# One 512 KB block of expert weights kept in two PSUM banks, in a decoder layer with 32 experts on Trainium2

## The reference

```
h2 = rms_norm(x) * norm2_w
logits = h2 @ w_router + b_router          # 32 experts
top 4 experts of each token, softmax over their logits
for each expert e, for the tokens that chose it:
    u = h @ w1[e] + b1[e]                  # w1: 1024 x 2048, 8 MB
    gate, lin = halves of u;  gate = min(gate, 7);  lin = clip(lin, -7, 7)
    y = (gate * sigmoid(1.702 * gate) * (lin + 1)) @ w2[e] + b2[e]    # w2: 1024 x 1024, 4 MB
    acc[token] += weight of the expert * y
out = rms_norm(x + acc) * final_norm_w
```

## Time and profile before

| | |
|---|---|
| median of 3 runs | 1038.2 us (1037.85 to 1038.82) |
| the profiled execution's own time | 1038.53 us |
| its span in the profile | 1036.7 us |
| moved by DMA | 424.64 MB, 410 GB/s over the span |
| granted clock of TensorE | 0.999 of full speed |

### The profile page before, as it was taken

How to read it: one execution, slowest core, us unless ns; L and a number is a source line. 1 busy time by engine, 2 the same in 40 slices (tenths; PEclk the granted TensorE clock), 3 DMA queues, 4 the chain that set the end, 5 groups by cost and what they waited for, 6 DMA issues and landing times.

```text
span 1036.7 us, 11300 instructions
## 1 busy us (share of the span) xinstructions
PE 1018.4 (98%) x4892; PEld 410.9 (40%) x4892; DVE 245.9 (24%) x613; ACT 126.6 (12%) x247; POOL 0.2 (0%) x4
## 2 busy tenths in 40 slices
PE   9999999999999999999999999999999999999996
PEld 8888443333333333333333333333333333333331
DVE  5776332111111111111111111110111111111111
ACT  2433120000000000000000000000000000000002
POOL 0000000000000000000000000000000000000000
PEclk9999999999999999999999999999999999999999
DMA  9983999999999999999999999999999999999995
GB/s 327 365 335 143 419 386 425 427 428 429 430 428 436 430 427 433 433 426 432 433 429 429 437 428 428 435 429 429 432 432 428 433 433 428 430 435 422 429 421 223
DMA packets 35976, 424.64 MB, mean 410 GB/s; under 512 B 3176, under 2 KB 16112, under 8 KB 19280
## 3 DMA queue, kind: packets, MB, share of 16 engines
q1 hardware_dynamic: 35616, 423.51, 97.0%
q10 hardware_dynamic: 304, 0.33, 0.1%
HBM read 422.78 MB, written 1.05 MB: 409 GB/s over the span
## 4 chain that ended last, share of the span: by engine, by line
PE 89%; DMA 9%; DVE 0%; another core or an unknown queue 0%; issue 0%; ACT 0%; DVEq 0%
PE PS L1861 39%; PE PS L1884 19%; DMA ring<-in_w 9%; PE PS L1455 6%; PE PS L1829 5%; PE PS L1811 5%; PE PS L1698 3%; PE PS L1658 3%; PE PS L1919 2%; PE PS L1821 2%; PE PS L1421 1%; PE PS L1803 1%; PE PS L1398 0%; PE PS L1991 0%; PE PS L2005 0%
## 5 line engine op out<-in xcount | busy, mean ns | idle before, releaser
L1861 PE MATMUL PS<-ring,work 128*64 128x512 f32 x1976 | 432.4, 594 | 6.6 <-DMA ring<-in_w 6.4
L1861 PEld LDWEIGHTS PS<-ring,work 128*64 128x64 f32 x1976 | 139.8, 137 | 276.2 <-issue 264.7
L1884 PE MATMUL PS<-ring,work 128*64 128x512 f32 x1024 | 227.6, 596 | 1.6 <-DMA ring<-in_w 1.5
L1884 PEld LDWEIGHTS PS<-ring,work 128*64 128x64 f32 x1024 | 72.3, 137 | 154.0 <-issue 150.0
L1301 DVE TENSOR_SCALAR work<-PS 128x512 f32<-128x512 f32 x32 | 22.1, 692 | 384.9 <-PE PS L1861 384.9
L842 ACT ACTIVATE work<-work 128x512 f32<-128x512 f32 x32 | 20.2, 630 | 523.0 <-DVE work L1301 523.0
L1266 DVE TENSOR_TENSOR work<-PS,n2w 128x512 f32<-128x512 f32 x30 | 20.7, 691 | 228.1 <-PE PS L1821 228.1
L1455 PE MATMUL PS<-ring 128*128 128x256 f32 x280 | 64.5, 382 | 0.0
L1829 PE MATMUL PS<-late,work 64*128 64x512 f32 x248 | 61.9, 616 | 0.0
L1811 PE MATMUL PS<-resid,work 128*64 128x512 f32 x248 | 58.5, 592 | 0.0
L1455 PEld LDWEIGHTS PS<-ring 128*128 128x128 f32 x280 | 51.8, 190 | 7.7 <-issue 1.3
(11 more groups left out here) (198 smaller groups left out, 455.7 us busy)
## 6 DMA issues: line engine op xcount, KB each, us to landing
ring<-in_w SPq DMA_DIRECT2D x72, 4096.0 KB, 35.7
ring<-in_w SPq DMA_DIRECT2D x35, 2048.0 KB, 13.1
ring<-in_w SPq DMA_DIRECT2D x22, 1024.0 KB, 8.4
ring<-in_w_in SPq DMA_DIRECT2D x11, 1024.0 KB, 12.1
ring<-in_w_out SPq DMA_DIRECT2D x4, 1024.0 KB, 11.1
ring<-in_w SPq DMA_DIRECT2D x6, 512.0 KB, 6.9
work<-in_w SPq DMA_DIRECT2D x1, 1024.0 KB, 9.0
out<-resid SPq DMA_DIRECT2D x3, 256.0 KB, 3.0
```

What stands on the lines that cost most here:

```text
L1861: last = mm(bank(b0 + v)[64 * half:64 * half + 64, :], rows[:, c, :], turned_half(w[:, v * F:(v + 1) * F], half), start=(second and c == 0 ...
L1884: last = mm(out[64 * half:64 * half + 64, :], aT_n[:, c, 64 * h:64 * h + 64], ring[:, 2 * d + c // 2, cols:cols + BANK], start=(h == 0 and ...
```

## The change

ScalarE copies the first 1024 columns of slot 7 (a part of g15, loaded ahead) to the PSUM banks 7 and 6. SP then loads the first 1024 columns of g16 (step 3, expert 3's w1) into that place of slot 7. When the first 1024 columns of g4 have been used, ScalarE copies the parked columns from PSUM to the first 1024 columns of slot 8, which before the change was the target of this part of g16. TensorE reads each from its new place: in `up` for g16, in `down` for g15. Chunk g27, which takes pair 3 (slots 6 and 7), waits for g16 in place of g15. To leave the banks 6 and 7 idle, the logits of the second tile go to bank 3 and the second half of the rows to bank 5. The two semaphores of the rows' copies become one.

```diff
@@ -60,10 +60,12 @@
 END_HALVES = [(LAST, W1_CHUNKS), (LAST, W1_CHUNKS + 1), (E, 0)]
 assert PEEL + ITERS * UNROLL + 2 == E and TURNS * PAIRS == UNROLL * STEP_CHUNKS
 SENTINEL = 3.0e38
-LT_BANK, LOGIT_BANK = (3, 0), (2, 6)
-ROWS0_BANK, TURN0_BANK = (4, 7), (3, 5)
+LT_BANK, LOGIT_BANK = (3, 0), (2, 3)
+ROWS0_BANK, TURN0_BANK = (4, 5), (3, 5)
+PARK_BANK = (7, 6)
 CUTS = {0: (1024, 2048), 1: (2048,), 2: (2048,), 3: (2048,), 4: (1024, 2048), 5: (2048,), 8: (2048,), 10: (2048,)}
 MOVED, AHEAD = 3, 3 + PAIRS
+GUEST, HOST = 4 + PAIRS, 4
 DEAL = 4
 WARM_X, WARM_WIN = 26, 12
 WIN0_PARTS, X_TURN_AT = [(0, 2), (2, C // 2)], C - 1
@@ -291,6 +293,8 @@
         y_last = g_sb
         gx = g_sb
         moved_w = work[:, 1280:3328]
+        lodging = ring[:, 2 * MOVED + 1, 0:2 * BANK]
+        parked_home = ring[:, 2 * HOST, 0:2 * BANK]
         y_sb = late[:, :]
         gh1 = late[:, :].rearrange("p (c s) -> p c s", c=C)
 
@@ -313,6 +317,8 @@
         early_in = {g: sem(f"early_in{g}") for g in CUTS if g != MOVED}
         moved_in = sem("moved_in")
         ahead_in = sem("ahead_in")
+        parked = sem("parked")
+        restored = sem("restored")
         x_in = [sem(f"x_in{k}") for k in range(T + 1)]
         cst_in = sem("cst_in")
         ident_in = sem("ident_in")
@@ -398,8 +404,7 @@
         pick0_ready = sem("pick0_ready")
         prefix0_done = sem("prefix0_done")
         rows0_done = sem("rows0_done")
-        rows0a_ready = sem("rows0a_ready")
-        rows0b_ready = sem("rows0b_ready")
+        rows0_ready = sem("rows0_ready")
         gather0_done = sem("gather0_done")
         rows_done = sem("rows_done")
         rows_ready = sem("rows_ready")
@@ -419,7 +424,6 @@
         fnw_mixed = sem("fnw_mixed")
         scaled = sem("scaled")
         combined = sem("combined")
-        final_ready = sem("final_ready")
         out_ready = sem("out_ready")
 
         read = {}
@@ -585,6 +589,8 @@
             sp.wait_ge(logits_done, T)
             sp.wait_ge(chunk_used, HEAD_CHUNKS)
             sp.dma_start(moved_w, moved_src).then_inc(moved_in, 16)
+            sp.wait_ge(parked, 2)
+            sp.dma_start(lodging, w1_half(3, 0)[:, 0:2 * BANK]).then_inc(early_in[HOST], 16)
 
             def load_ahead_rest(j, k):
                 sp.wait_ge(early_used, cut_count(MOVED, 0))
@@ -597,8 +603,9 @@
                 dst = ring[:, 2 * d:2 * d + 2, :].rearrange("p a n -> p (a n)")
                 at = 0
                 for n, cut in enumerate(CUTS[freed]):
-                    sp.wait_ge(early_used, cut_count(freed, n))
-                    sp.dma_start(dst[:, at:cut], src[:, at:cut]).then_inc(early_in[freed], 16)
+                    if freed != HOST or n > 0:
+                        sp.wait_ge(early_used, cut_count(freed, n))
+                        sp.dma_start(dst[:, at:cut], src[:, at:cut]).then_inc(early_in[freed], 16)
                     at = cut
                 sp.wait_ge(chunk_used, HEAD_CHUNKS + freed + 1)
                 sp.dma_start(dst[:, at:], src[:, at:]).then_inc(pair_full[d], 16)
@@ -625,8 +632,9 @@
                         sp.wait_ge(chunk_used, r * ROUND_CHUNKS + HEAD_CHUNKS)
                     else:
 
+                        freed = GUEST if isinstance(r, int) and g == AHEAD + PAIRS else g - PAIRS
                         sp.wait_ge(chunk_used, r * ROUND_CHUNKS + i * (UNROLL * STEP_CHUNKS)
-                                   + (HEAD_CHUNKS + g - PAIRS + 1))
+                                   + (HEAD_CHUNKS + freed + 1))
                     load(r, i, j, k)
 
             run_experts(sp, step_loads, 0)
@@ -814,10 +822,13 @@
                                  ACT.Copy).then_inc(h2T1a_ready, 1)
             square_x2(1, 1, 4)
             std_x2(1)
+            act.wait_ge(ahead_in, 16)
+            for n, b in enumerate(PARK_BANK):
+                nc.scalar.activation(bank(b), lodging[:, half_cols(n)], ACT.Copy).then_inc(parked, 1)
             for a in range(2):
                 act.wait_ge(rows0_done, a + 1)
                 nc.scalar.activation(gx1[0:64, a * SEQ:(a + 1) * SEQ], bank(ROWS0_BANK[a])[0:64, 0:SEQ],
-                                     ACT.Copy).then_inc(rows0a_ready, 1)
+                                     ACT.Copy).then_inc(rows0_ready, 1)
             for t in range(T):
                 act.wait_ge(top_ready, t + 1)
                 nc.scalar.activation(expl[:, t, :], logits[:, t, 0:E], ACT.Exp,
@@ -840,6 +851,10 @@
                 if j < E:
                     act.wait_ge(gate_ready, n + 1)
                     nc.scalar.activation(s_sb, g_sb, ACT.Sigmoid, scale=ALPHA).then_inc(sig_ready, 1)
+                if isinstance(r, int) and j == 0:
+                    act.wait_ge(early_used, cut_count(HOST, 0))
+                    for h, b in enumerate(PARK_BANK):
+                        nc.scalar.activation(parked_home[:, half_cols(h)], bank(b), ACT.Copy).then_inc(restored, 1)
                 if j < LAST and not (isinstance(r, int) and j == 0):
                     take_rows(n + 1)
                 if j == LAST:
@@ -1326,7 +1341,7 @@
 
                 dve.wait_ge(rows0_done, a + 1)
                 nc.vector.tensor_copy(gx1[64:P, a * SEQ:(a + 1) * SEQ],
-                                      bank(ROWS0_BANK[a])[64:P, 0:SEQ]).then_inc(rows0b_ready, 1)
+                                      bank(ROWS0_BANK[a])[64:P, 0:SEQ]).then_inc(rows0_ready, 1)
 
             def take_gather0(half, a):
 
@@ -1791,8 +1806,7 @@
             for a in range(2):
                 gather0_rows(1, a).then_inc(rows0_done, 1)
             bias0_part(1).then_inc(bias_done, 1)
-            pe.wait_ge(rows0a_ready, 2)
-            pe.wait_ge(rows0b_ready, 2)
+            pe.wait_ge(rows0_ready, 4)
             for a in range(2):
                 turn_rows0(a)
 
@@ -1854,8 +1868,10 @@
                         moved = first and q == MOVED and c % 2 == 1
                         if moved:
                             pe.wait_ge(moved_in, 16)
-                        w = moved_w if moved else ring[:, 2 * d + c % 2, :]
                         for v in range(2):
+                            w = moved_w if moved else ring[:, 2 * d + c % 2, :]
+                            if isinstance(r, int) and g == GUEST and c % 2 == 0 and v == 0:
+                                w = lodging
                             for half in range(2):
                                 at = v * F + half * BANK
                                 last = mm(bank(b0 + v)[64 * half:64 * half + 64, :], rows[:, c, :], turned_half(w[:, v * F:(v + 1) * F], half),
@@ -1875,14 +1891,15 @@
                         transpose_gates()
                         bias(1, 2, False)
 
-            def down_part(j, k, c0, c1, aT_n, out):
+            def down_part(j, k, c0, c1, aT_n, out, lodged=None):
 
                 d, h = pair_of(j, k), down_chunk(j, k)
                 for c in range(c0, c1):
                     for half in range(2):
                         cols = (c % 2) * D + half * BANK
+                        w = parked_home if c == lodged else ring[:, 2 * d + c // 2, :]
                         last = mm(out[64 * half:64 * half + 64, :], aT_n[:, c, 64 * h:64 * h + 64],
-                                  ring[:, 2 * d + c // 2, cols:cols + BANK],
+                                  w[:, cols:cols + BANK],
                                   start=(h == 0 and c == 0), stop=(h == 1 and c == 3))
                 return last
 
@@ -1898,7 +1915,8 @@
                     down_part(j, k, 0, 2, aT, bank(5)).then_inc(early_used, 1)
                     down_part(j, k, 2, 4, aT, bank(5)).then_inc(chunk_used, 1)
                     return
-                down_part(j, k, 0, 4, aT, bank(5)).then_inc(chunk_used, 1)
+                lodged = 2 if isinstance(r, int) and g == AHEAD else None
+                down_part(j, k, 0, 4, aT, bank(5), lodged).then_inc(chunk_used, 1)
 
             def down_first(r, j, k):
 
@@ -1993,6 +2011,7 @@
 
             def transpose_gates():
                 pe.wait_ge(most_ready, 1)
+                pe.wait_ge(restored, 2)
                 for t in range(T):
                     last = nc.tensor.transpose(bank(7)[0:E, t * P:(t + 1) * P], gates[:, t, 0:E], ident)
                 last.then_inc(gatesT_done, 1)
```

## The result

The changed kernel takes 1041.02 us (median of 12 runs, 1040.39 to 1042.84) against 1038.22 for the kernel before (12 runs beside it, 1037.72 to 1039.86). The ratio is 1.0022, with a 95% interval of 1.0014 to 1.0029: 2.3 us slower by the ratio (1.5 to 3.0), 2.8 by the medians. The forecast was 1040.9, a loss of 2.7.

A forecast was written before the change was run, and what follows sets the result against it. The prediction took the loads of weights (DMA time) to set the end. Its terms, 0 for parking, return, banks and SP plus 2.7 us for the late g27, gave 1041.2, or 1040.9 us against the runs' median; range 1038.9 to 1041.9.

The forecast's parts named there:

- my three rows: 2 MB landings into an idle queue: 7.2 us (at 100.9), 8.1 (at 131.2), 7.9 (built from 66.9); 7.7 taken.
- Parts 1 and 3: ScalarE's two parking copies near 133.5 us and two return copies near 157, covered by idle time or slack: 0.
- Part 5: After g28 the DMA queue has work to the end, so the 2.7 us loss stays; TensorE catches up before 808.
- The chain's long piece of loads: Sign in the changed kernel's profile: it begins before 808 us and the last weights land near 1020.3.
- Part 2: SP's early 512 KB load at about 134.9 us fills the dip at 141: 0 to 1.23 us earlier behind it.
- part 4: g27 issued at 216.69, 7.3 us late, empties the queue; g28 lands 2.7 us late, bounds 2.2 and 3.1.
- The first rival: At the wait of g27, an idle queue lands 2 MB nearer 7.0 us: loss 2.0, 1040.2 us; chance 0.11.
- The other rivals: At g27: the 1.2 us gain kept, 1037.0 us, chance 0.05; or the late load hidden, 1038.2, chance 0.06.

The follow-up runs named there:

- the repeat: The changed kernel run and profiled once more, against the kernel before: 1040.69 us, ratio 1.0016.
- late1: The kernel before with one line changed, g27 waiting for g16 in place of g15, nothing parked: 1040.63 us, ratio 1.0018.
- split_cols: The changed kernel with g27 loaded in three parts, only the 512 KB under g16's borrowed place waiting for its matmuls: 1038.75 us, ratio 0.9999; once more 1038.3, 0.9997.
- guest_cols: The changed kernel with g27 waiting only for the first four matmuls of g16, which read the borrowed place: 1039.38 us, ratio 1.0004.
- copies: The changed kernel without the early load and the later wait of g27; parking, return and moved banks stay: 1038.64 us, ratio 1.0002.
- more halves: The kernel split_cols with g18, g19, g21 and g23 also issued in two 1 MB halves: 1038.72 us, ratio 0.9998 against the kernel before.
- drop: The kernel before without the 512 KB load of g16's first 1024 columns at 156.5 us: 1038.16 us, ratio 0.9993.
- Extra: The kernel copies with an additional early 512 KB load that nobody reads, g16 still loaded whole later: 1038.23 us, ratio 0.9997 against the kernel before.

## Why the prediction was right

**Right in the cause, and in the sum within its bounds.** The forecast was one term, 2.7 us with bounds of 2.2 and 3.1, at one wait, that of g27. Measured are 2.3 us by the ratio (1.5 to 3.0), and 1.7 in the repeat (0.6 to 2.6); the wait alone (late1) makes 1.9, a longer wait 6.1, and without the wait (split_cols) nothing is left of the loss. The landing of a 2 MB load into an idle queue took 7.2 us, in the repeat too, which is the lowest of my three rows and not the 7.7 I took. That is the row at 100.9 us, the one with the emptiest queue, which was the nearest case. With it the prediction's sum gives 2.2 us, and g28 lands 2.3 late.

The fixed part beyond the 4.9 us of transport is thus 2.3 us. The Trainium skill ("DMA: Bandwidth & Descriptors", the anatomy of one DMA) gives about 2.0 for DMAs of the GpSimd path, while these are issued by SP; the 1.8 us of loss that I estimated from it are 0.5 short of the landing and within the intervals of the times.

That g28's landing and the ratio agree at 2.3 is in part luck. The prediction took the lateness of one landing for the loss. In the repeat 3.3 us of transport are missing in the gap, g31 lands 3.2 us late and the last weights 2.4; in guest_cols g28 is 2.2 late and the time 0.4. So the price lies between 2.3 and 3.3 us of transport by the traces and near 2 by the times. Why the later landings differ from that of g28, and where up to 1 us of the missing transport goes before the end, isn't shown.

**Parts 1 and 3 at zero**: right (copies, 1.0002; 1.10 and 1.07 us of copies, nothing moved behind them). **Part 5**, that the end is set by the loads: right, and by how much is now known, about 10 us of TensorE work. The chain's long piece of loads began before 808 us in the repeat (781.63) and not in the first profile (834.52), where a slower clock had put TensorE behind.

**Wrong in parts 2 and 4, on what the guest brings.** Part 2 has everything behind the guest up to 1.23 us earlier, and part 4 checks the way at one place: the load of 192.8 lands with 1.5 us to spare, "so 1.23 us ahead opens no gap there". No gap opened in the share, and yet the gain was given back, most of it before that load was issued (174 to 182 us): the rate fell from 426 to between 404 and 412 GB/s in all five profiles of kernels with a guest and g16's usual issues, to 405 with more halves too, and to 411 in drop. It made no difference to the sum, since the gap at 216 would have taken the gain in any case. It does decide what the idea is worth: with the wait repaired, twice nothing that can be told from zero (0.9999 and 0.9997), where by my part 2 it would have been up to 1.2 us. None of the versions beats the kernel before beyond its interval.

**The chances.** The first rival, "the restart is quick", had as its condition a landing nearer 7.0 than 7.7 us, and the 7.2 that was measured meets it. I had given it 0.11, too little. Its price of 2.0 us and the forecast's 2.7 both lie within 1.5 to 3.0, so the times don't tell them apart, and the forecast's 1040.9 against 1041.02 is closer than the method allows. The other rivals fell by their own places: the gain was not kept, and the loss was not hidden.

**Open.** Why packets already take longer while the landings, by my measure, still have 1.5 us to spare. Extra and drop show that it hangs on the bytes taken out at 156.5, and the durations of the packets show where the time goes; what an engine waits for within such a packet they don't show. A kernel with enough halves to reach all the short places (174 to 198 us) wasn't tried.

## What to carry to other kernels

Where the DMA time sets the end, count what a change does to each issue, not only to the bytes: a borrowed place must be given back before its next load is due, and one load held back 7.3 us was enough to empty a queue whose last transfer still had 7.5 us to its landing (209.39 to 216.85). To see whether an early transfer is a gain, look at the depth of the queue all the way to where it is safe, because time filled at 141 us was lost again by 200 us. When the queue is shallow, read the rate and not the share.

## What was not expected of the hardware

A DMA share of 1.01 goes with 426 GB/s in one kernel and with 404 in another, over the same 42 us and loads of the same sizes. A share near 1 is no proof that nothing is lost. And in the changed kernel g26 was still landing while the share was 0.04 (218 to 219 us): its issue at 207.87 took 11.8 us, to 219.67, which is 0.9 us later than in the kernel before by the shifted times, though the engines had been mostly idle for 2 us. The repeat doesn't show this delay (206.14 + 11.0 = 217.1, 216.9 with its start taken off, for 216.85 before), so it belongs to that execution. The landing is the moment at which the last of the 16 engines is done, and says nothing of the others.
